# Mixture-of-experts block on one core: the experts with two blocks at places 3, 10, 17 and 24, and the table products ahead of the first gate-up

## What is computed

```
logits = xt @ router_w + router_b
top_v, top_e = lax.top_k(logits, 4)
wts = softmax(top_v)
...
def expert_block(args):
    xb, e = args
    hgu = xb @ w_gate_up[e] + b_gate_up[e]
    gate, up = jnp.split(hgu, 2, axis=-1)
    gate = jnp.minimum(gate, 7.0)
    up = jnp.clip(up, -7.0, 7.0)
    act = (up + 1.0) * (gate * jax.nn.sigmoid(1.702 * gate))
    return act @ w_down[e] + b_down[e]
```

## Time and profile before

| | us |
|---|---|
| median of 3 runs | 1381.20 |
| lowest, highest | 1380.29, 1381.88 |
| profiled execution, its own time | 1381.2 |
| its span (first to last instruction) | 1379.5 |
| PE busy in the span | 1339.8 (97%) |
| POOL busy | 710.9 (52%) |
| DVE, ACT busy | 412.0 (30%), 234.7 (17%) |
| HBM read | 483.44 MB, 352 GB/s over the span |

### The profile page before, as it was taken

The page is one execution under the profiler, slowest core; times in us unless marked ns, Lnnn a source line. Parts: engine busy times, 40 slices in busy tenths (PEclk is TensorE's granted clock), DMA queues, the critical chain, the costliest instruction groups (busy, mean ns, idle before and its releaser), DMA issues.

```text
span 1379.5 us, 17459 instructions
## 1 busy us (share of the span) xinstructions
PE 1339.8 (97%) x6442; PEld 624.2 (45%) x6443; DVE 412.0 (30%) x755; ACT 234.7 (17%) x401; POOL 710.9 (52%) x425
## 2 busy tenths in 40 slices
PE   5999999999999999999999999999999999999996
PEld 2888545788743333333333333333333333333332
DVE  2160015355664331113321322312232231231222
ACT  2320004310023111111211211211211211211202
POOL 0000000000013777768777677777677776777773
PEclk9899999999999999999999999999999999999999
DMA  9735342599757999999999989999899998999995
GB/s 351 252 123 183 122 138 106 190 324 362 275 227 308 431 428 429 429 399 420 428 429 429 427 365 428 430 427 429 363 429 429 427 429 362 430 429 427 431 427 221
DMA packets 70914, 485.89 MB, mean 352 GB/s; under 512 B 7254, under 2 KB 7418, under 8 KB 45450
## 3 DMA queue, kind: packets, MB, share of 16 engines
q1 hardware_dynamic: 69490, 480.56, 85.1%
q0 software_dynamic: 1056, 3.93, 1.0%
q10 hardware_dynamic: 344, 1.07, 0.2%
HBM read 483.44 MB, written 2.10 MB: 352 GB/s over the span
## 4 chain that ended last, share of the span: by engine, by line
PE 70%; DMA 26%; DVE 1%; issue 1%; POOL 1%; SPq 1%; ACT 1%; DVEq 0%; POOLq 0%; ACTq 0%
PE bank L1600 22%; DMA landing<-in_w_gate_up 17%; PE bank L1261 15%; PE bank L1647 12%; DMA landing<-in_w_down 7%; PE bank L1270 6%; PE bank L1579 4%; PE bank L1617 2%; PE bank L1496 2%; DMA piece<-in_w_ada 1%; PE bank L1634 1%; PE bank L1544 1%; POOL gu_slot L527 1%; PE bank L1607 1%; PE bank L1630 1%
## 5 line engine op out<-in xcount | busy, mean ns | idle before, releaser
L527 POOL COPY gu_slot<-landing 128x2048 f32<-128x2048 f32 x248 | 463.0, 1898 | 196.7 <-issue 117.5
L1600 PE MATMUL bank<-gu_slot,xg 128*64 128x512 f32 x2304 | 510.7, 593 | 8.8 <-POOL gu_slot L527 7.9
L1600 PEld LDWEIGHTS bank<-gu_slot,xg 128*64 128x64 f32 x2304 | 162.4, 137 | 329.0 <-issue 295.8
L527 POOL COPY dn_slot<-landing 128x2048 f32<-128x2048 f32 x124 | 231.3, 1897 | 76.3 <-issue 55.5
L1647 PE MATMUL bank<-dn_slot,actT 128*64 128x512 f32 x1152 | 255.1, 595 | 0.0
L1647 PEld LDWEIGHTS bank<-dn_slot,actT 128*64 128x64 f32 x1152 | 79.5, 137 | 171.2 <-issue 171.2
L1261 PE MATMUL bank<-hT,piece 128*128 128x256 f32 x704 | 155.1, 382 | 0.0
L1170 DVE TENSOR_SCALAR bank<-bank 128x512 f32<-128x512 f32 x36 | 25.2, 699 | 399.2 <-PE bank L1600 399.2
L1261 PEld LDWEIGHTS bank<-hT,piece 128*128 128x128 f32 x704 | 134.5, 192 | 19.6 <-issue 1.1
L744 ACT ACTIVATE sig<-bank 128x512 f32<-128x512 f32 x36 | 21.5, 598 | 696.7 <-PE bank L1600 696.7
L1180 DVE TENSOR_TENSOR ysb<-bank,gt2q 128x512 f32<-128x512 f32 x36 | 24.9, 692 | 253.7 <-PE bank L1647 253.7
(11 more groups left out here) (323 smaller groups left out, 902.7 us busy)
## 6 DMA issues: line engine op xcount, KB each, us to landing
landing<-in_w_gate_up SPq DMA_DIRECT2D x124, 2048.0 KB, 10.7
landing<-in_w_down SPq DMA_DIRECT2D x62, 2048.0 KB, 10.7
piece<-in_w_in SPq DMA_DIRECT2D x17, 2048.0 KB, 8.7
piece<-in_w_ada SPq DMA_DIRECT2D x12, 2048.0 KB, 13.1
gu_slot<-in_w_gate_up SPq DMA_DIRECT2D x8, 1024.0 KB, 7.3
piece<-in_w_branch_a SPq DMA_DIRECT2D x2, 2048.0 KB, 9.2
dn_slot<-in_w_down SPq DMA_DIRECT2D x4, 1024.0 KB, 11.3
piece<-in_w_branch_b SPq DMA_DIRECT2D x2, 2048.0 KB, 8.7
```

What stands on the lines that cost most here:

```text
L527: nc.gpsimd.tensor_copy(place, landing[j // 2 % 3][:, j % 2, :]).then_inc(there, 16)
L1600: ins = M(gu_bank[u][64 * q:64 * q + 64, :], xg[:, k % 4, 64 * (k // 4):64 * (k // 4) + 64], gu_slot[k][:, cols_], start=(k == 0), stop=(k ...
```

## The change

Two edits. First, `place_of` is written with steps of seven: ranks 0 to 4 stand at places 3, 10, 17, 24, 31, the next four at 7, 14, 21, 28, then 5, 12, 19, 26, and so on; rank 31 stays at place 0. POOL has one iota more. Second, the table products and the copy of the table move ahead.

```
-            for first, n in ((6, 5), (3, 5), (5, 5), (2, 5), (1, 6), (4, 5), (0, 1)):
+            for first, n in ((3, 5), (7, 4), (5, 4), (1, 5), (2, 5), (4, 4), (6, 4), (0, 1)):
                 step.settle()
-                step(nc.gpsimd.iota(place_of[:, at:at + n], [[6, n]], base=first, channel_multiplier=0,
+                step(nc.gpsimd.iota(place_of[:, at:at + n], [[7, n]], base=first, channel_multiplier=0,
...
             step(V.scalar_tensor_tensor(of_block[:], iota[0:3 * E, 0:MAXB + 1], end_col[:], started[:], ALU.is_lt, ALU.mult),
                  places_ready)
 
+            wait_tile(dve, "te")
+            chain(V.tensor_copy(table[:], tile("te")[0:1, 0:ends[5]]), tables_ready)
             for t in range(TT):
                 dve.wait_ge(rexp_ready, t + 1)
...
-            wait_tile(dve, "te")
-            chain(V.tensor_copy(table[:], tile("te")[0:1, 0:ends[5]]), tables_ready)
             select_weights(None)
...
             wait_out(pe, "br")
-            gate_up(16, 1, (block_tables, weight_transposes))
+            block_tables()
+            gate_up(16, 1, (lambda: None, weight_transposes))
             pe.wait_ge(tables_ready, 1)
```

## The result

In the first comparison the changed kernel took 1368.21 us (median of 4 executions, 1366.83 to 1370.71) and the kernel before 1381.43 us (4 executions, 1380.29 to 1381.88): a ratio of 0.9908, with a 95% interval from 0.989 to 0.9926. The profiled execution of the changed kernel took 1370.71 us, with a span of 1369.0.

The account below looks back on a forecast made before the run. PE and the DMA both run near their limit; PE waits for weights, and the stream stops at two-block experts. Places 9.6 plus stream start 0.25 gave 9.85 us: 1381.2 - 9.9 = 1371.3 us, range 1369.4 to 1373.3.

Parts of the forecast that it names:

- the term of the places: Mixture, places 3 to 31: PE's waits of 10.8 us become 1.2, a gain of 9.6 us, bounds 9.1 to 10.0.
- the 9.85 of the sum: Whole kernel: 9.6 us from the places plus 0.25 from the stream's earlier start, bounds 8.9 and 11.0.
- Both rivals on the price of a stop: Stream at extra blocks: fixed stop of 5.3 to 5.4 us; 1384.3 us (4%), or 1381.0 with place 3 cheap (4%).
- The rival of PE never waiting: Behind place 3 PE's four waits vanish: 11.05 us gained, 1370.1 us; chance 8%.
- the price of 4.81 us for a unit: Weight stream: the Trainium skill's estimate per 2 MB unit, 28.9 us per expert; no waits at places 10 to 31.
- the tables: Mixture start: table ready about 2.2 us earlier, PE cost 0 to 0.2, stream's start 0.25 us earlier, bounds 0 and 0.97.
- the base of the sum: Kernel before: 1381.2 us, its profiled execution and median of its runs, from which 9.9 us were subtracted.
- The range: Whole kernel: 1369.4 to 1373.3 us, from the sum's bounds, the first rival and some 0.8 us of run spread each side.

Follow-up runs that it names:

- the places alone: The kernel before with only the new table of places, table products and table copy left where they stood; median 1367.93 us, ratio 0.9927 to the kernel before.
- eight places: The changed kernel with the two-block experts at places 3, 11, 19 and 27; median 1379.52 us, ratio 1.0005 to the kernel before.
- the one with five places: The changed kernel with the two-block experts at places 3, 8, 13 and 18; median 1387.38 us, ratio 1.0074 to the kernel before.
- the third profile of the changed kernel: The changed kernel, unchanged, run a third time beside the dense-front kernels; median 1368.81 us, ratio 0.9936 to the kernel before.
- the tables alone: The kernel before with only the table products and table copy moved ahead, places as before; median 1378.58 us, ratio 1.0009 to the kernel before.

## Why the prediction was right and wrong

**Right: what bounds the kernel, and the term of the places.** The forecast for the mixture was that 10.8 us of PE's waits become 1.2, bounds 0.8 to 1.7. Measured: 0.87, and stops of the stream of 8.2 where 8.0 to 9.2 stood. The down products of the last block begin 10.1 us earlier, between the 9.85 of the sum and its upper bound of 11.0. The arithmetic behind it (25.93 us per extra block, 3.44 made up per place, room for about 23.7, which is seven times 3.44 less the wait of 0.42 in the last block of the kernel before) then gave the waits at two new distances before they ran: 3.64 for 3.7 and 20.9 for 21. Both rivals on the price of a stop fall with it: no stop behind place 3 costs 5.3. The rival of PE never waiting falls too: it waits at each of the four places, though for the lower of the two values between which 0.3 was chosen. With it falls the price of 4.81 us for a unit, at which PE would have waited at none of them; the stream's 29.37 us for an expert, 4.90 for a unit, held in the changed kernel too (29.35 between the units 0 of places 6 and 7, issued at 572.38 and 601.73).

**Right in kind, small in size: the tables.** PE lost nothing, the table came 2.3 us earlier (2.2 forecast), unit 0 was issued at 421.42 (421.5), and the stream moved by 0.14 (0.25). With the places alone the time is the same. So this half of the change does nothing that can be measured. One thing behind it had not been foreseen, and is told below.

**Wrong: the base of the sum.** The step that failed is "the profiled execution took 1381.2, which is also the median of the runs: 1381.2 - 9.9", with its "some 0.8 us to both sides for the spread of the runs". Three executions within 1.6 us were taken for the kernel's spread. It is 1375.7 to 1381.7 over 56 executions, median 1377.6, and only 11 of these 56 reach the 1380.29 from which all four of the first comparison go up. The trace of the kernel before even showed where the time goes, half clock from 28.8 to 39.1 and 56.1 to 59.6 us, and I did not ask whether every execution has it. The page of the profile gives it as one digit, an 8 in the second slice. With a base of 1377.6 the same sum gives 1367.7, and the 16 executions of the changed kernel have a median of 1368.3. Put the other way: of the 13.2 us that the first comparison showed, some 10 are the change. The other 3 come from which executions were taken: all four executions of the kernel before came from the upper part of its times while those of the changed kernel were spread over theirs. (The range also has a slip of 0.2 us: its own terms, 1372.3 and 0.8, give 1373.1 and not 1373.3. It changes nothing here.)

**Open.** Why all four of the first comparison fell into the upper group, where a fifth of the later ones do, is not known; the chip of that comparison isn't on record, nor is the clock of the kernel before in it, other than the 0.993 of its profiled execution. Nor is it shown what decides in an execution where the half clock falls. That it falls at different places in one program is shown. Filling PE's pauses didn't remove the scatter, in four kernels; whether it moved the half clock can't be told, since that lies elsewhere from one execution of the plain kernel to the next as well.

## What to carry to other kernels

Where a transfer stream with little buffer room is slower than a unit of work, and a few units come double, write down three numbers: what a double unit puts the engine behind, what is made up at each step, and what the buffers hold. The doubles belong at the distance at which the second has just used up the third, not closer (the stream stops) and not wider (the engine waits), and the first of them where the engine first catches up. And before a forecast of 0.7% is given a range of 0.3%, ask what the executions of one kernel differ by: compare at the same mean clock, compare the stretch of the trace that the change concerns, or run each kernel ten times or more.

## What the runs showed of the hardware

One program on one core of one chip took from 1375.96 to 1381.68 us, with mean granted clocks from 0.997 down to 0.992. The half clock came in stretches of 3.4, 10.2 or 13.7 us at different places of the dense part: from 28.8 to 39.1 and 56.1 to 59.6 in four profiles (the kernel before, the changed one, the places alone, eight places), from about 27 to 30.5 in three others, in two of these with another stretch from 416 to 419.6, from 26.9 to 37.2 in the one with five places, and in the third profile of the changed kernel only from 53.1 to 56.6. Ahead of the fall at 28.8 PE had short pauses and one-column products (L1289). They can't be the whole cause: the third profile of the changed kernel has the same pauses and products there and keeps the full clock up to 53.1, and with wide products in these pauses the clock fell in some executions as well. Nor does it take a pause: ahead of the fall at 56.1 in the changed kernel PE is busy without one by the profile, for 12.00 of the 12.00 us from 40 to 52 and for 8.00 of the 8.00 us behind.

A surprise behind the table edit: DVE's two selections (L1132) took 3.70 us in the changed kernel where they took 0.42 before (L1130). The timeline of DVE before, then those of DVE and POOL in the changed kernel:

```profile
429.45 0.42 DVE L1130 TENSOR_SCALAR pick<-iota,slot_id 128x64 bf16<-128x64 f32 x2
...
429.32 3.70 DVE L1132 TENSOR_SCALAR pick<-iota,slot_id 128x64 bf16<-128x64 f32 x2
...
429.24 3.72 POOL L527 COPY gu_slot<-landing 128x2048 f32<-128x2048 f32 x2 [33.69 <-DMA landing<-in_w_gate_up]
```

Unit 0 comes earlier now, so that POOL's two copies (429.24 to 432.96) lie over the two selections. The two half changes separate it: with the places alone the selections take 0.42 us and POOL's copies begin at 431.28, behind them; with the tables alone they take 3.68 us (from 425.03) under copies of 3.72 (from 424.94). The group's mean, 824 ns for one selection in the changed kernel against 731 before, doesn't tell it: it is 798 with the places alone, and the two selections make 3.3 of the 6.5 us between the sums of the first two. The Trainium skill has a rule for it, "SBUF — State Buffer", in the part on the two sides and their ports: VectorE and GpSimd share one pair of SBUF ports as an exclusive lock; a GpSimd instruction and a VectorE instruction that uses both ports (in a 2-port mode, or with two inputs in SBUF) take it for their whole length, and the later one blocks. The trace agrees in this: POOL's copy begins 0.08 us before the first selection, and the two selections are each as long as one copy of POOL (3.70 / 2 = 1.85 and 3.72 / 2 = 1.86). That the selection ran in such a mode is not shown. It cost nothing: what is selected is needed at 434.59 only, when PE ends the gate-up.
